# Thirteen gather slots or seventeen: `w_out` half resident and half loaded per tile, and projection units moved behind the first gather

## The reference

```python
proj = h @ w_in                                # RMSNorm(x) W_in, 2824 columns
x = x + jnp.concatenate([hm, hs], -1) @ w_out  # mLSTM heads | sliding-window heads
# peer, per block of 128 rows
q = (xb @ w_q).reshape(TB, 8, 256)
s1, s2 = scores of both halves of q against 128 sub-keys each
idx = 16 best of the 16 x 16 candidates per head
g = softmax(top)
u = jnp.take(expert_u, idx, axis=0)            # rows of 1024
a = gelu(einsum('thkd,td->thk', u, xb))
y = einsum('thk,thkd->td', g * a, jnp.take(expert_v, idx, axis=0))
```

## Time and profile before

| | |
|---|---|
| median of 3 runs | 3126.98 us (3126.38 to 3129.21) |
| profiled execution, span | 3386.3 us |
| the profiled execution's own time outside the span | not given; the span is used |
| TensorE, VectorE, POOL, ScalarE busy | 77%, 63%, 59%, 16% |
| mean granted TensorE clock | 0.81 of full speed |
| moved by DMA | 1197 MB, 353 GB/s |

### The profile page before, as it was taken

The page is one execution under the profiler, slowest core; times in us unless marked ns, Lnnn a source line. Parts: engine busy times, 40 slices in busy tenths (PEclk is TensorE's granted clock), DMA queues, the critical chain, the costliest instruction groups (busy, mean ns, idle before and its releaser), DMA issues.

```text
span 3386.3 us, 33673 instructions
## 1 busy us (share of the span) xinstructions
PE 2600.2 (77%) x10989; PEld 1007.2 (30%) x10989; DVE 2120.6 (63%) x5282; ACT 556.3 (16%) x1093; POOL 1995.2 (59%) x2128
## 2 busy tenths in 40 slices
PE   8996886678678899987876876678676776686666
PEld 4562351225222533223432331124212331121101
DVE  1256657766676666657667757676667666676653
ACT  2211111211121131122012111111111011111001
POOL 0026556666666566665656666666666666666665
PEclk9997897789677899997987887788667886677667
DMA  6479999999999999999999999999999999999998
GB/s 230 146 275 371 336 338 374 362 371 343 378 351 365 342 400 407 409 382 353 362 329 346 380 354 381 367 364 345 384 360 360 370 365 376 358 368 370 371 363 332
DMA packets 348919, 1197.02 MB, mean 353 GB/s; under 512 B 37760, under 2 KB 54408, under 8 KB 346952
## 3 DMA queue, kind: packets, MB, share of 16 engines
q0 software_dynamic: 304128, 1107.43, 86.7%
q1 hardware_dynamic: 44616, 87.45, 7.0%
HBM read 1180.69 MB, written 14.15 MB: 353 GB/s over the span
## 4 chain that ended last, share of the span: by engine, by line
PE 33%; DVE 16%; issue 13%; POOL 12%; DMA 9%; another core or an unknown queue 8%; DVEq 6%; ACT 1%; ACTq 0%; SPq 0%; POOLq 0%
PE acc L1657 11%; PE mx L1549 7%; DVE ring L1261 7%; POOL ring L593 6%; POOL ring L582 6%; DMA ring<-in_peer_v_dram,idx 5%; DVEq L1148 4%; DMA ring<-in_peer_u_dram,idx 4%; PE mx L1365 3%; PE mx L1531 2%; PE acc L1341 2%; PE mx L1560 2%; PE acc L1328 1%; PE h2p L1603 1%
## 5 line engine op out<-in xcount | busy, mean ns | idle before, releaser
L1657 PE MATMUL acc<-ring,wk 128*32 128x512 f32 x4224 | 1362.6, 742 | 525.6 <-DMA ring<-in_peer_v_dram,idx 289.4
L1261 DVE SCALAR_TENSOR_TENSOR ring<-ring,h2p 128x1024 f32<-128x1024 f32 x1056 | 1273.8, 1215 | 565.4 <-DMA ring<-in_peer_u_dram,idx 315.8
L593 POOL DMA_INDIRECT ring<-in_peer_v_dram,idx x1056 | 997.1, 944 | 707.7 <-issue 269.7
L582 POOL DMA_INDIRECT ring<-in_peer_u_dram,idx x1056 | 996.3, 943 | 667.1 <-issue 292.9
L1657 PEld LDWEIGHTS acc<-ring,wk 128*32 128x32 f32 x4224 | 217.8, 122 | 1406.6 <-issue 670.8
L1549 PE MATMUL mx<-reg,weights 128*128 128x128 f32 x1792 | 256.7, 297 | 40.9 <-issue 38.6
L1549 PEld LDWEIGHTS mx<-reg,weights 128*128 128x128 f32 x1792 | 230.8, 206 | 145.7 <-issue 145.7
L1531 PE MATMUL mx<-weights,reg 128*128 128x512 f32 (+1 forms) x256 | 133.0, 643 | 3.5 <-issue 3.5
L1365 PE MATMUL mx<-weights 128*128 128x512 f32 (+1 forms) x288 | 126.9, 585 | 0.0
L821 ACT ACTIVATE gl<-dots 128x16 f32<-128x16 f32 x66 | 14.2, 216 | 637.5 <-issue 346.1
L1603 PE MATMUL h2p<-ch,ident 32*32 32x512 f32 x528 | 86.7, 708 | 36.6 <-issue 18.9
(11 more groups left out here) (310 smaller groups left out, 2400.3 us busy)
## 6 DMA issues: line engine op xcount, KB each, us to landing
ring<-in_peer_u_dram,idx POOLq DMA_INDIRECT x1056
ring<-in_peer_v_dram,idx POOLq DMA_INDIRECT x1056
weights<-in_peer_w_q_dram SPq DMA_DIRECT2D x7, 2048.0 KB
weights<-in_w_in_dram SPq DMA_DIRECT2D x5, 2048.0 KB, 18.2
weights<-in_w_in_dram SPq DMA_DIRECT2D x10, 1024.0 KB
ring<-in_peer_w_q_dram SPq DMA_DIRECT2D x8, 1024.0 KB, 5.6
xt<-in_x_prompt_dram SPq DMA_DIRECT2D x8, 512.0 KB
ring<-in_w_out_dram SPq DMA_DIRECT2D x2, 2048.0 KB, 14.2
```

The source lines that it names most:

```text
L582: pool.indirect_dma_start(ring[:, n % NU, :], None, u_d, bass.IndirectOffsetOnAxis(ap=idx[:, g % 4, k:k + 1], axis=0)).then_inc(u_in[n % N ...
L593: pool.indirect_dma_start(ring[:, NU + n % NV, :], None, v_d, bass.IndirectOffsetOnAxis(ap=idx[:, g % 4, k:k + 1], axis=0)).then_inc(v_in[ ...
L1261: V.scalar_tensor_tensor(ring[:, n % NU, :], ring[:, n % NU, :], 1.0, h2p[:, :], ALU.mult, ALU.mult, accum_out=dots[:, (g + 1) % 2, k:k + ...
L1657: last = T.matmul(acc[j:j + SUB, cols], wk[:, g % 2, n % TOPK, :], ring[:, NU + n % NV, cols], start=g % 2 == 0 and n % TOPK == 0, stop=g ...
```

## The change

- `w_out`: only the first `WK` = 4 of 8 k slices stay resident. For each tile 1 to 8 the other four are loaded again (`pass_wout`): three of them, once the attention's output is there, into `pj` and the upper half of `reg`, the last, once the mixer's rows are transposed, into `ch[m % 2]`. `out_proj` takes the resident slices first and waits for the three at its step 2 and for the last at its step 7.
- Slots: the 4 x 1024 columns that come free in `weights` become one more slot for U (7) and three more for V (10).
- Units: `BEHIND` is 7, number 7 comes behind `out_proj`, 8 to 11 stand in slots -16 to -7, and 12 to 17 (`LATE`) in slots 1 to 13 beside the first V products, in banks of `mx`, and over new staging buffers in `reg`. The first V product waits for the copies of units 0 to 11. The piece of `w_q` that was loaded before the first gather is loaded after unit 11; tile 1's mixer begins at slot 16 + 0.61 r (before: -4 + 0.85 r).

The heart of the diff:

```diff
-NU = 6
-NV = 7
+RU, RV = 6, 7
+NU = 7
+NV = 10
+WK = 4
...
-EARLY_AT = ((10, 0), (14, 2), (20, 4), (24, 6), (32, 7), (36, 9), (46, 11), (50, 14), (54, 15), (EARLY_END, 16))
-UNITS = [(c, m) for c in range(3) for m in range(1, FIRST)]
+EARLY_AT = ((10, 0), (14, 2), (20, 3), (24, 5), (32, 6), (36, 8), (46, 9), (50, 11), (54, 12), (EARLY_END, 13))
+UNITS = [(c, m) for c in range(2) for m in range(1, FIRST)] + [(2, 1)]
 BEHIND = len(UNITS)
-UNIT_PE = {-16: 10, -14: 11, -12: 12, -10: 13, -8: 14, -6: 15, -4: 16, -2: 17}
+LATE = 12
+UNIT_PE = {-16: 8, -13: 9, -10: 10, -7: 11, 1: 12, 3: 13, 6: 14, 8: 15, 11: 16, 13: 17}
...
     if m == 1:
-        return -4 + r * 85 // 100
+        return 16 + r * 61 // 100
...
-        wout_s = weights[:, 0:DC * D].rearrange("p (k c) -> p k c", k=DC)
+        wout_s = weights[:, 0:WK * D].rearrange("p (k c) -> p k c", k=WK)
-        ring = sb("ring", [P, NU + NV, D])
+        ring = sb("ring", [P, RU + RV, D])
+        spare = [weights[:, (WK + i) * D:(WK + i + 1) * D] for i in range(NU - RU + NV - RV)]
+        u_slot = [ring[:, b, :] for b in range(RU)] + spare[:NU - RU]
+        v_slot = [ring[:, RU + b, :] for b in range(RV)] + spare[NU - RU:]
...
+        wout_pass = [pj[:, 0:D], pj[:, D:2 * D], reg[:, D:2 * D]]
...
-        unit_bank = [acc[:, 0:512], acc[:, 512:1024]]
+        unit_bank = [acc[:, n % 2 * 512:n % 2 * 512 + 512] if n < LATE else mx[:, n % 2, :] for n in range(len(UNITS))]
...
+            def pass_wout(m):
+                sp.wait_ge(attn_ready, m + 1)
+                for j in range(3):
+                    k = WK + j
+                    sp.dma_start(wout_pass[j], w_out[0, k * P:(k + 1) * P, :]).then_inc(wout_pass_in, 16)
+                sp.wait_ge(rows_transposed, 2 * m + 1)
+                sp.dma_start(ch[m % 2][:, :], w_out[0, (DC - 1) * P:DC * P, :]).then_inc(wout_last_in, 16)
...
                 if m != FIRST:
                     load_p(m)
+                pass_wout(m)
                 store_y(m - 2)
...
+                    if m > 0 and i == WK // 2:
+                        pe.wait_ge(wout_pass_in, 16 * 3 * m)
+                    if m > 0 and i == DC - 1:
+                        pe.wait_ge(wout_last_in, 16 * m)
...
                 elif q == 0:
-                    pe.wait_ge(chunk_act, 3 * FIRST)
-                    pe.wait_ge(chunk_dve, 3 * FIRST)
+                    pe.wait_ge(chunk_act, 3 + LATE // 2)
+                    pe.wait_ge(chunk_dve, 3 + LATE // 2)
```

More of the change, by code:

```diff
@@ L291, in program @@
         po = [sc[:, 4 * b:4 * b + 4, :].rearrange("p c k -> p (c k)") for b in range(4)]
-        po += [part[:, :]] + [ring[:, NU + 4, 0:512]] + [a[:, h * 512:h * 512 + 512] for a in (ring[:, NU + 5, :], ring[:, NU + 6, :]) for h in range(2)]
+        po += [part[:, :]] + [ring[:, RU + 4, 0:512]] + [a[:, h * 512:h * 512 + 512] for a in (ring[:, RU + 5, :], ring[:, RU + 6, :]) for h in range(2)]
+        po += [reg[:, 512 * i:512 * i + 512] for i in range(4)]
         first = [pj[:, 0:512], pj[:, 512:1024], vx[:, :, 0:MD], pj[:, 1024:1536], pj[:, 1536:2048], pj[:, 2048:PJ]]
@@ L313, in program @@
         chunk_act, chunk_dve = sem("chunk_act"), sem("chunk_dve")
-        proj_out = [sem(f"proj_out{b}") for b in range(10)]
+        proj_out = [sem(f"proj_out{b}") for b in range(14)]
         wout_in, wq_in = sem("wout_in"), sem("wq_in")
+        wout_pass_in, wout_last_in = sem("wout_pass_in"), sem("wout_last_in")
         keysT_ready, keysT_copied = sem("keysT_ready"), sem("keysT_copied")
@@ L522, in _ @@
             load_x(1)
-            for b in range(10):
+            for b in range(14):
                 sp.wait_ge(proj_out[b], stored(b, len(UNITS)))
+            pass_wout(1)
             for m in range(2, TILES):
@@ L589, in gather_v @@
                     pool.wait_ge(v_free, n - NV + 1)
-                elif n >= NV - 3:
-                    for b in {NV - 3: (5,), NV - 2: (6, 7), NV - 1: (8, 9)}[n]:
+                elif RV - 3 <= n < RV:
+                    for b in {RV - 3: (5,), RV - 2: (6, 7), RV - 1: (8, 9)}[n]:
                         pool.wait_ge(proj_out[b], stored(b, len(UNITS)))
-                pool.indirect_dma_start(ring[:, NU + n % NV, :], None, v_d,
+                pool.indirect_dma_start(v_slot[n % NV], None, v_d,
                                         bass.IndirectOffsetOnAxis(ap=idx[:, g % 4, k:k + 1], axis=0)).then_inc(v_in[n % NV], 16)
@@ L714, in mix @@
                     act.wait_ge(qk_transposed, m + 1)
+                    if m == 1:
+                        for b in range(10, 14):
+                            act.wait_ge(proj_out[b], stored(b, len(UNITS)))
                     S.copy(qkT[:, 0:4, 0:n], mx[:, 2, :].rearrange("p (h t) -> p h t", h=4)[:, :, 0:n])
@@ L1006, in mix @@
                     dve.wait_ge(qk_transposed, m + 1)
+                    if m == 1:
+                        for b in range(10, 14):
+                            dve.wait_ge(proj_out[b], stored(b, len(UNITS)))
                     V.tensor_scalar(qkT[:, 4:8, 0:n], mx[:, 3, :].rearrange("p (h t) -> p h t", h=4)[:, :, 0:n], MD ** -0.5, None, ALU.mult)
@@ L1260, in _ @@
                     dve.wait_ge(u_in[n % NU], 16 * (n // NU + 1))
[L1261 removed]
+                    V.scalar_tensor_tensor(u_slot[n % NU], u_slot[n % NU], 1.0, h2p[:, :], ALU.mult, ALU.mult,
                                            accum_out=dots[:, (g + 1) % 2, k:k + 1]).then_inc(u_free, 1)
@@ L1340, in project_unit @@
                     for k in range(4 * half, 4 * half + 4):
-                        last = T.matmul(unit_bank[n % 2][:, 0:PC[c][1]], hT1[m][:, k, :], win_s[c][:, k, :], start=k == 0, stop=k == DC - 1)
+                        last = T.matmul(unit_bank[n][:, 0:PC[c][1]], hT1[m][:, k, :], win_s[c][:, k, :], start=k == 0, stop=k == DC - 1)
                     if half == 1:
@@ L1520, in mix @@
                 elif s == "out_proj":
-                    half, k0 = i // 4, i % 4 * 2
+                    pairs = [(i // 4, i % 4 * 2 + a) for a in range(2)]
+                    if m > 0:
+                        pairs = [divmod(2 * i + a, DC - 1) for a in range(2)] if i < DC - 1 else [(0, DC - 1), (1, DC - 1)]
                     if i == 0:
@@ L1527, in mix @@
                     if m == 0 and i % 4 == 0:
-                        pe.wait_ge(wout_first_in[half], 16)
-                    for k in (k0, k0 + 1):
-                        w = wout_first[half][:, k, :] if m == 0 else wout_s[:, k, half * 512:half * 512 + 512]
+                        pe.wait_ge(wout_first_in[i // 4], 16)
+                    if m > 0 and i == WK // 2:
+                        pe.wait_ge(wout_pass_in, 16 * 3 * m)
+                    if m > 0 and i == DC - 1:
+                        pe.wait_ge(wout_last_in, 16 * m)
+                    for half, k in pairs:
+                        cols = slice(half * 512, half * 512 + 512)
+                        if m == 0:
+                            w = wout_first[half][:, k, :]
+                        elif k < WK:
+                            w = wout_s[:, k, cols]
+                        else:
+                            w = (wout_pass + [ch[m % 2][:, :]])[k - WK][:, cols]
                         last = T.matmul(mx[0:n, 2 + half, :], t8[:, k, 0:n], w, start=k == 0, stop=k == DC - 1)
```

31 lines of the change are left out of this document (18 added, 13 removed).

## The result

| | before | changed |
|---|---|---|
| median of 4 runs | 3126.68 us (3123.40 to 3129.21) | 3156.19 us (3152.90 to 3158.76) |
| ratio | | 1.0093 [1.0081, 1.0106] |
| profiled execution, span | 3386.3 us | 3155.6 us |
| moved by DMA | 1197 MB, 353 GB/s | 1212 MB, 384 GB/s |

The account below looks back on a forecast made before the run. The prediction took no engine or DMA to be saturated: POOL, VectorE and TensorE run into each other through 13 slots. -13 - 10 + 31 + 3 - 60 = -49 us, -1.4%, carried to 3127 us: 3082 us; range 3005 to 3150.

Parts of the forecast that it names:

- 326 us are lost to gaps: Gather loop, 312 to 3340 us: 1105 MB at 365 GB/s would take 2702 us at 409, so 326 us are lost.
- I carry the share over: Sum of -49 us on the profiled 3386.3 us, -1.4%, applied as a share to the median, giving 3082 us.
- part 4: Gather loop: 17 slots instead of 13 let gathers wait for older products, -60 us; bounds 0 and -160.
- the long window: Sign in the gather loop, 312 to 3340 us before: 365 GB/s should rise to 370 to 378 if the forecast is right.
- Rival B: DMA transfers are the limit already: slots bring 0, reload bytes cost their full 46 us; sum +26, 3151 us; chance 0.16.
- parts 1 and 2: Program start: two units fewer before the first gather, -13 us; first V products earlier, with units between them, -10 us.
- The form 409 N/(N + k): Gather rate against slots N, k = 1.57 from 365 GB/s at 13; 15 to 17 slots give 370 to 374, -43 to -76 us.
- TensorE and VectorE also stop each other directly: Gather loop: reason to cap the slots' gain at half of the 326 us, -160; VectorE stood 57 us for h2's spread.
- V waits of POOL under 403 us and U waits above 157: Signs of a right forecast: POOL's slot waits before V gathers well under 403 us, before U gathers above 157.
- Part 3: Half of w_out reloaded for each of 8 tiles, 16.8 MB: 0.75 of 41 us, +31 us; bounds 0 and 46.
- The late `w_out` (+3): out_proj of tiles 1 and 4, with only 6 and 7 slots for the load, waits for w_out: +3 us, bounds 0 and 15.
- the 19 us stop: Start: POOL stands 19.19 us at V gathers whose slots hold staged projections; the forecast had this stop go.

Follow-up runs that it names:

- units_only: Only the moved units of the change, w_out whole and resident, 6 and 7 slots: 3420.4 us, 1.0012; repeated as units_only_b in session 2: 3134.4 us, 1.0016 against the kernel before.
- traffic_13: The change (moved units, w_out reloads) with 6 and 7 slots instead of 7 and 10: 3419.3 us, 1.0005 against the kernel before in session 1.
- units_back: The change with units, tile 1's mixer and early w_q load at their old places: 3485.6 us, 1.0277 against the kernel before (3393.3 us).
- ring_old_units: 17 slots alone: units at old places, no reloads, half of w_out never used: 3480.3 us, 1.0260 against the kernel before (3393.3 us).
- again_before: The kernel before, unchanged, measured again in session 1: 3414.6 us, ratio 0.9999.
- u7_v6: The kernel before with its 13 slots split 7 for U and 6 for V, instead of 6 and 7: 3388.8 us, 0.9913 against the kernel before (3414.7 us).

## Why the prediction was wrong

**What bounds the kernel: the step that failed first.** "326 us are lost to gaps" was not true of the runs, and only about half true of the profile: its DMA share of 0.97, against 1.03 in the full windows, leaves by my estimate 6% of 3028 us, some 176 us, in which the queues stood empty. The rest of the 326 are packets that took longer, as the last section counts, and no slot shortens those. The text had the warning: an execution 8.3% longer than the median, and 383 GB/s in the runs. It answered with "I carry the share over". But the 8.3% were not a stretch of everything: they were the gaps and slow packets that part 4 lived on. At the 3127 level 13 slots give 397 GB/s (units_only_b), so 3% were to be had in the best case. This could be worked out beforehand: the page's mean of 353 GB/s stands to the runs' 383 as the long window's 365 to 396. The forecast should have put the sum on that. Rival B was this case, with 3151 against 3156.2 measured; its parts were not right, since it had -23 for the units and 0 for the slots, and its errors cancel.

**Part 4, -60 us: -12 measured at the 3127 level.** This is the term that makes most of the miss, 48 us; parts 1 and 2 make 28 more. The form 409 N/(N + k) was fitted at 365 GB/s. Fitted at 397 it has k = 0.39, and 13 to 17 slots would be 397 to 400 GB/s, 20 us on 2788; 399 and -12 were measured. And where the gaps were real, at the 3400 level, the form gives the wrong sign: 7 and 10 slots cost 2.2%. A count of slots was the wrong variable. The sentence "TensorE and VectorE also stop each other directly" came near the mechanism, and then I let it only cut the gain in half. The signs that I had named, V waits of POOL under 403 us and U waits above 157, both came true and told nothing: they follow from the split of the slots, whether the queues have gaps or not. The sign that told was the long window, 401 GB/s for 370 to 378.

**Part 3, +31 us: +30.3 and +30.1 measured**, so three quarters of the 41 us that 16.8 MB take. Beside 13 slots the pair of kernels differs by 14.7 MB only, since `units_only` loads all of `w_out` at the start; beside 17 slots it is 16.8 MB, and the cost is the same. The match is partly luck: the 0.75 was read from a profile of the 3400 level, and there the same bytes cost -1 us (traffic_13 less units_only) and +5 (units_back less ring_old_units), nothing that those runs can tell. The late `w_out` (+3) didn't show: TensorE has no such wait, and the slices land 7.4 to 11.1 us (medians) after their issue.

**Parts 1 and 2, -23 us: +5.4 measured at the 3127 level, +3 at the other** (there inside the noise). Most of their times came out: first gather at 180 to 184.5 in all profiles with the moved units (192 to 194.5 without), forecast 179; first V product at 227; the 19 us stop gone. What was wrong is that this gain lasts. Session 1 has both kernels on one chip, windows of `again_before`, then of `units_only`:

```profile
170.00:370.00 200.00, 155.41 (x763) 81.50 (x762) 127.38 (x367) 34.66 (x72) 94.58 (x101) 0.83 0.88 327
370.00:530.00 160.00, 134.41 (x746) 66.47 (x744) 103.34 (x248) 22.69 (x34) 95.73 (x103) 0.89 0.94 347
```

```profile
170.00:370.00 200.00, 161.10 (x691) 72.77 (x691) 132.12 (x373) 30.38 (x55) 103.21 (x108) 0.85 0.91 349
370.00:530.00 160.00, 129.84 (x726) 66.44 (x722) 95.38 (x234) 28.11 (x52) 84.77 (x90) 0.85 0.84 296
```

By 370 us POOL has done 108 instructions, nearly all of them gathers, for 101, and by 530 us 198 for 204. Tile 1's mixer, in 57 slots instead of 79, gives back all of it: 296 for 347 GB/s. The prediction named the squeeze and gave it no price of its own. (That it is the squeeze, and not the load of `w_q` or the late units in this stretch, is not shown: no run moved one of them alone.) That the same stretch takes the gain at the 3127 level is likely (319 GB/s from 400 to 500 us in units_only_b, the lowest of its 100 us windows after the start), but there is no profile of before at that level to compare with, so it stays open.

**The rule of the Trainium skill** (DMA: Bandwidth & Descriptors, "Where 436 GB/s comes from"; about 358 GB/s per core on the HBM side) pointed to the rival whose time came nearest, B. Its number isn't that of the runs: 401 GB/s for 2788 us, 415 at best. The 361 to 365 of the 3400 level look like it, but there too single stretches reach 405 to 412.

**The chances.** 0.16 for B was too low. With 560 us of slot waits in the profile I read POOL's waits as proof of slack; the changed kernel has 454 us of such waits at 401 GB/s. A producer that waits for slots says only that it is ahead.

## What to carry to other kernels

When the profiled execution is some per cent longer than the timed ones, work out the rate that the bottleneck has in the timed runs (bytes by median, scaled as above) and price every gain against that rate, for a gap that exists only in the profile can't be won. In a loop with one in-order producer and two in-order consumers, try the split of the slots before their number: at the 3400 level one slot moved from V to U was worth 26 us, and four added to the wrong side cost 5%. At the 3127 level the split wasn't tried. Work that leaves the head of the program comes back where it is put; price the stage that is squeezed to make room.

## What was not expected of the hardware

- Two levels, 3127 and 3393 to 3421 us, for one binary. The mean granted clock of the kernel before differs little (0.83 to 0.85, and 0.80 to 0.82). Counted over the records of the gathers' 4 KB packets, the median is 0.160 us at the first level and 0.159 at the second, but packets over 0.3 us are 0.6 to 0.7% at the first and 2.2 to 2.8% at the second. Taken over 16 engines, their excess over 0.16 us is 38 to 48 us and 153 to 195 us, about half of the difference between the levels; most of the rest is time in which the queues stood empty (DMA share 0.96 to 0.97 for 1.01), and whether the long packets bring that about isn't shown. The long ones come in bursts, and in sessions of the second level at the same gathers (correlation 0.55 to 0.68 over groups of 512 packets between profiles of the kernel before). They don't hang on the rows fetched alone: `u7_v6` fetches the same rows in the same order, and its correlation with them is 0.34 to 0.41. Why one session has them and another not is open, and nothing in the records tells whether something outside the program was at work.
- The reloads (16.8 MB, 14.7 more in all) cost 30 us at the 3127 level and nothing measurable at the 3400 level.
